# One core's decoder trunk: the compressed branch's pieces between the attention's groups, transposes at the changes of stage, and transfers in smaller pieces

## The chip, the cores and the metric

The kernel runs on one core of a Trainium2 chip. Its engines work side by side and wait for each other through semaphores: TensorE (PE; its weight loads are listed as PEld), VectorE (DVE), ScalarE (ACT), GpSimd (POOL) and SyncE (SP), which here only issues transfers. ACT issues transfers too. The metric is the device time of one execution in microseconds (us). TensorE's clock is granted by a throttle at one of two levels; the profile gives it as a share of full speed (PEclk).

## The reference

One layer on 512 prompt tokens and 8 sequences of 8 sample tokens, in float32: a half-step feed-forward layer (FFN), a mixer, a second half-step FFN, each between two RMS norms.

```
x = x + 1/2 * post1(SwiGLU_1(pre1(x)))
u = pre_m(x) @ w_in            # q, kv of three kinds, gates, z, xbc, dt
a = NSA(q, kv, gates)          # compressed + selected + window attention, gated
s = SSD(z, xbc, dt)            # causal convolution, chunked scan, grouped norm
x = x + post_m(concat(attn_norm(a), s) @ w_out)
x = x + 1/2 * post2(SwiGLU_2(pre2(x)))
```

The compressed branch (`compress_blocks` with the weights `w_cmp`) makes one key and one value of each block of 64 tokens; its softmax is added to the result of the two other branches. For the samples keys and values come from paged caches.

## The kernel before, in words

`x` is held transposed in `xT` (features on partitions, 8 chunks `k` of 576 tokens). Every float32 product of the large layers is made of three products of rounded parts: ACT writes the high part of an operand (rounded), VectorE subtracts it from the operand to get the low part, PE multiplies high by high, high by low and low by high (`product`, L490).

The stages follow each other, each a block of instruction streams, one per engine, in an order written by hand; a block begins when all engines have ended the one before. `setup` loads constants and pages of the sample's cache and compresses the pages (L399; a page is a transfer of 256 KB in rows of 2 KB, and the weights `w_cmp` come whole in two transfers of 2 MB in rows of 32 KB, L291 and L311). `ffn` is called twice; pieces of the weights are loaded to a ring, rounded by ACT (L750) and finished by VectorE (L811). `mixer_in` has two blocks: the first makes keys, values and gates (L984 to L1016), the second q, xbc and z. Then come `ssd`, `attend_prompt`, `attend_sample` and `mixer_out`.

Where a stage ends with a norm, the sum of squares is finished by the next stage: `tail.post.total` (L517) on PE, the root by ACT as Ln and Exp (L535 to L541), then for each chunk VectorE's `tail.scale` (L553) and `tail.add` (L558), ACT's rounding (L1034, L763) and VectorE's low part (L1057, L815), which PE waits for. VectorE's order there is scale 0, scale 1, add 0, scale 2, add 1, low part 0, and so on.

At the end of `mixer_in` VectorE copies the last rows of the convolution (L1279), which SP sends out. At the end of `ssd` SP sends the last state (L1376) and waits until it has landed.

`attend_prompt` has a prelude and a loop over 32 groups (kv head, branch, 128 queries). The prelude holds the lengths of the SSD rows, the compress of the prompt's keys and values, and the whole compressed branch: scores, a turn of them, softmax on VectorE and ACT, a turn of the shares, and products with the values (L1939), which are the first contents of the result `onat`. In the loop PE makes scores, turns them and multiplies by values; VectorE scales the result of a group to `tmp`, and POOL adds it to `onat`.

`mixer_out` begins with ACT's length of an attention row (L2737) and the rounding of the SSD rows and of the first weights (L2731, L2727; VectorE L2775, L2770).

## Time and profile before

| | |
|---|---|
| median of 3 runs | 1972.95 us (1970.59 to 1973.65) |
| profiled execution | 1965.59 us, span of its instructions 1963.7 |
| mean granted clock of TensorE | 0.947 |
| transfers | 189.15 MB, 96 GB/s in the mean |

The span is the time from the first to the last instruction of the profiled execution. Busy time counts an engine's arithmetic alone. A wait is put down to what ended it. "issue" and "PEq" as the releaser mean that no other engine's work or transfer was seen to end the wait, as with a barrier between blocks. A matmul's duration includes the way through the array, so that durations of neighbours overlap.

### The profile page before, as it was taken

The page shows a single profiled execution, that of the slowest core. Times are in us where ns is not written, and L with a number is a line of the kernel's source. Part 1 is how long each engine was busy: PE and PEld are TensorE (multiplying, and loading weights), DVE is VectorE, ACT ScalarE, POOL GpSimd, SP SyncE. Part 2 cuts the span into 40 slices and gives each one's busy share as a digit, 9 for nine tenths or more (in the row PEclk, how much of TensorE's full clock was granted, in tenths as well). Part 3 has the DMA queues.
Part 4 walks back from the last instruction along what each step waited for, and adds up shares of the span by engine and source line. Part 5 has one row for each costly group of instructions (what it writes and reads, how often), then busy time and mean ns, then how long its engine had stood idle before and what let it go on. Part 6 is the DMA issues. An engine that isn't in the chain of part 4 may idle for free. (4 is left out here: it accounts for less than half of the span.)

```text
span 1963.7 us, 36443 instructions
## 1 busy us (share of the span) xinstructions
PE 1772.0 (90%) x15067; PEld 1670.4 (85%) x15067; DVE 789.3 (40%) x1460; ACT 605.2 (31%) x967; POOL 111.9 (6%) x141
## 2 busy tenths in 40 slices
PE   3899999999978989997976999788897899999997
PEld 2789999999978989996755888666896899999996
DVE  3123443432242124744555555443525344443223
ACT  0122222222133212223434776243523322222222
POOL 0000000000000000101200111333000000000000
PEclk9899999999989989997977999899898999999998
DMA  9703444342311332321242002465320222223221
GB/s 252 272 26 116 145 150 152 112 121 76 88 48 44 92 92 75 86 54 40 83 124 71 23 23 65 145 200 151 102 86 22 65 85 85 85 85 95 78 84 48
DMA packets 256209, 189.15 MB, mean 96 GB/s; under 512 B 29604, under 2 KB 227744, under 8 KB 255299
## 3 DMA queue, kind: packets, MB, share of 16 engines
q1 hardware_dynamic: 248184, 173.43, 30.2%
q10 hardware_dynamic: 7916, 14.18, 2.5%
q8 instruction: 79, 1.29, 0.3%
q14 instruction: 30, 0.25, 0.0%
HBM read 176.14 MB, written 24.81 MB: 102 GB/s over the span
## 5 line engine op out<-in xcount | busy, mean ns | idle before, releaser
L490 PE MATMUL PS<-f_x_h,f_w_h 128*128 128x288 f32 x1408 | 303.6, 297 | 21.8 <-DVE f_w_l L811 12.1
L490 PE MATMUL PS<-f_x_h,f_w_l 128*128 128x288 f32 x1408 | 300.9, 295 | 0.0
L490 PE MATMUL PS<-f_x_l,f_w_h 128*128 128x288 f32 x1408 | 300.9, 295 | 0.0
L490 PEld LDWEIGHTS PS<-f_x_h,f_w_h 128*128 128x128 f32 x1408 | 227.9, 190 | 24.7 <-DVE f_w_l L811 13.3
L490 PEld LDWEIGHTS PS<-f_x_l,f_w_h 128*128 128x128 f32 x1408 | 227.4, 190 | 0.0
L490 PEld LDWEIGHTS PS<-f_x_h,f_w_l 128*128 128x128 f32 x1408 | 227.2, 189 | 0.0
L750 ACT CAST f_w_h<-f_raw 128x1024 fp32r<-128x1024 f32 x88 | 92.1, 1048 | 412.7 <-PE PS L490 334.1
L490 PE MATMUL PS<-f_h_h,f_out_w_h 128*128 128x288 f32 x704 | 150.9, 296 | 0.0
L490 PE MATMUL PS<-f_h_l,f_out_w_h 128*128 128x288 f32 x704 | 150.7, 295 | 0.0
L490 PE MATMUL PS<-f_h_h,f_out_w_l 128*128 128x288 f32 x704 | 150.7, 296 | 0.0
L811 DVE TENSOR_TENSOR f_w_l<-f_raw,f_w_h 128x1024 fp32r<-128x1024 f32 x88 | 107.7, 1225 | 50.0 <-ACT f_w_h L750 50.0
L807 DVE TENSOR_TENSOR f_out_w_l<-f_out_raw,f_out_w_h 128x1408 fp32r<-128x1408 f32 x32 | 52.0, 1625 | 188.3 <-ACT f_out_w_h L744 188.3
L490 PEld LDWEIGHTS PS<-f_h_h,f_out_w_h 128*128 128x128 f32 x704 | 113.4, 189 | 0.0
L490 PEld LDWEIGHTS PS<-f_h_l,f_out_w_h 128*128 128x128 f32 x704 | 113.2, 188 | 0.0
L490 PEld LDWEIGHTS PS<-f_h_h,f_out_w_l 128*128 128x128 f32 x704 | 112.8, 188 | 0.0
L490 PE MATMUL PS<-mk_x_h,mq_w_h 128*128 128x288 f32 x448 | 97.1, 299 | 8.7 <-DVE mq_w_l L1199 8.7
L744 ACT CAST f_out_w_h<-f_out_raw 128x1408 fp32r<-128x1408 f32 x32 | 43.9, 1371 | 179.1 <-PE PS L490 168.1
L490 PE MATMUL PS<-mk_x_l,mq_w_h 128*128 128x288 f32 x448 | 96.7, 298 | 0.0
L490 PE MATMUL PS<-mk_x_h,mq_w_l 128*128 128x288 f32 x448 | 96.5, 297 | 0.0
L399 PE MATMUL PS<-arena 64*64 64x64 f32 (+2 forms) x1536 | 75.7, 376 | 21.4 <-DMA arena<-in_cache_cmp_kv 13.0
L843 DVE TENSOR_TENSOR f_silu<-PS,norm_rows 128x576 f32<-128x576 f32 x44 | 33.3, 756 | 147.8 <-PE PS L490 139.6
L399 PEld LDWEIGHTS PS<-arena 64*64 64x64 f32 x1536 | 69.2, 167 | 27.6 <-issue 23.6
(405 smaller groups left out, 3107.0 us busy)
## 6 DMA issues: line engine op xcount, KB each, us to landing
f_raw<-in_ffn_w_in SPq DMA_DIRECT2D x88, 512.0 KB, 3.9
f_out_raw<-in_ffn_w_out SPq DMA_DIRECT2D x32, 704.0 KB, 4.6
arena<-in_cache_slc_kv SPq DMA_DIRECT2D x64, 256.0 KB, 3.1
mq_raw<-in_w_in SPq DMA_DIRECT2D x20, 512.0 KB, 3.8
arena<-in_cache_cmp_kv SPq DMA_DIRECT2D x32, 256.0 KB, 13.5
arena<-in_cache_cmp_kv ACTq DMA_DIRECT2D x32, 256.0 KB, 13.2
arena<-in_cache_win_kv SPq DMA_DIRECT2D x8, 1024.0 KB, 7.1
mo_raw<-in_w_out SPq DMA_DIRECT2D x16, 512.0 KB, 3.7
```

The source lines that it names most:

```text
L399: m = pe.matmul(PS[col:col + 64, 2 + 2 * c + half, c0:c0 + n], wd[r, c * HD + d + odd, :], rhs, start=(d == 0), stop=(d == HD - 2))
L490: m = pe.matmul(PS[:, bank + half, 0:HALF], a[:, wk, :], b[:, xk, half * HALF:(half + 1) * HALF], start=start and j == 0, stop=stop and j ...
L744: act.copy(ow[s].h, pieces.raw[s]).then_inc(o_h[s], 1)
L750: act.copy(ws[side].h, raw[side]).then_inc(s_h[side], 1)
L807: dve.tensor_tensor(ow[s].l, pieces.raw[s], ow[s].h_f32, ALU.subtract).then_inc(o_l[s], 1)
L811: dve.tensor_tensor(ws[side].l, raw[side], ws[side].h_f32, ALU.subtract).then_inc(s_l[side], 1)
L843: dve.tensor_tensor(cut(silu[j]), both(4 * j), cut(rstd[:, :]), ALU.mult).then_inc(s_gate, 1)
```

## The change

It has these parts. A helper `keep_turning` lets PE transpose the identity into a bank of the accumulator memory that nobody reads: 25 times at the start of each FFN, 30 before the final transposes, 40 at the start and 25 at the end of `mixer_in`, 20 at the end of `ssd`, 25 at the end of `attend_sample` and 25 at the start of `mixer_out`. In setup the two transfers of `w_cmp` become sixteen. The order on VectorE at the start of the second FFN and of `mixer_in` becomes scale 0, add 0, scale 1, low part 0, and so on. The two blocks of `mixer_in` become one (its ACT and VectorE streams are joined; the variables of the second are renamed to `q_ws`, `q_mm`, `q_ev`), and the convolution's rows are copied after the third z step. The waits for outgoing data at the end of `ssd` and `attend_sample` move into the next stage. In `attend_prompt` the weights come in quarters, only the compress itself stays ahead of the loop, and the compressed branch's pieces stand at the ends of groups 0 to 30, all through the one bank `BK`. VectorE then writes the first branch of a group straight to `onat` (`results`), the second goes by POOL as before, and the compressed values are added by VectorE. The sample's score matmuls for the new columns take both branches at once. In `mixer_out` ACT rounds before it takes row lengths.

```diff
-                    sp.dma_start(wd[0:64, :, :], kh).then_inc(s_w, 16)
+                    for j in range(8):
+                        sp.dma_start(wd[0:64, 16 * j:16 * j + 16, :], kh[:, 16 * j:16 * j + 16, :]).then_inc(s_w, 16)
...
-                        act.dma_start(wd[64:P, :, :], kh).then_inc(s_w, 16)
+                        for j in range(8):
+                            act.dma_start(wd[64:P, 16 * j:16 * j + 16, :], kh[:, 16 * j:16 * j + 16, :]).then_inc(s_w, 16)
...
+
+        def keep_turning(pe, bank, n):
+
+            for _ in range(n):
+                pe.transpose(PS[:, bank, 0:P], ident, ident)
...
                     if tail is not None:
                         tail.post.total(pe)
+                    keep_turning(pe, 5, 25)
...
                     if last:
                         post_norm.total(pe)
+                        keep_turning(pe, 5, 30)
...
                         rest_of_piece(1, 0)
                     for k in range(KD if rows is None else 0):
                         if tail is None and k == 1:
                             rest_of_piece(1, 0)
                         if tail is not None:
-                            tail.scale(dve, k)
-                            if k:
-                                tail.add(dve, k - 1)
-                            if k > 1:
-                                rest_of_x(k - 2)
-                        else:
-                            rest_of_x(k)
-                    if tail is not None:
-                        tail.add(dve, KD - 1)
-                        for k in range(KD - 2, KD):
+                            if k == 0:
+                                tail.scale(dve, 0)
+                            tail.add(dve, k)
+                            if k == 0:
+                                rest_of_piece(1, 0)
+                                rest_of_x(0)
+                            if k + 1 < KD:
+                                tail.scale(dve, k + 1)
+                        if tail is None or k:
                             rest_of_x(k)
                     if pages is not None:
...
+        def load_cmp(eng, half, q):
             w = io["w_cmp"].rearrange("a l c d e -> (a l) (c d) e")
-            for q in range(2):
-                eng.dma_start(wd[64 * half:64 * half + 64, :, :].rearrange("p (c d) e -> p c d e", c=2)[:, :, 32 * q:32 * q + 32, :],
-                              w.rearrange("l (c d) e -> l c d e", c=2)[:, :, 32 * q:32 * q + 32, :]).then_inc(s_cmp_w[q], 16)
+            eng.dma_start(wd[64 * half:64 * half + 64, :, :].rearrange("p (c d) e -> p c d e", c=2)[:, :, 16 * q:16 * q + 16, :],
+                          w.rearrange("l (c d) e -> l c d e", c=2)[:, :, 16 * q:16 * q + 16, :]).then_inc(s_cmp_w[q], 16)
...
                 @block.tensor
                 def _(pe):
                     tail.post.total(pe)
+                    keep_turning(pe, 5, 40)
...
+                    keep_turning(pe, 7, 25)
...
+                    act.wait_ge(s_sw, 32)
+                    act.copy(sw.h, smw).then_inc(s_swh, 1)
+                    nrm.take_root(act, 4, KD)
+                    round_piece(1)
...
+                        if p + 2 < NP:
+                            round_piece(p + 2)
+                        if p == NP - 2:
+                            act.wait_ge(s_wl, NP)
+                            for s in range(2):
+                                round_chunk(s, 0, land_q[s], 32)
+                    act.dma_start(stn, io["state_conv"].rearrange("a b w n -> (a b w) n")).then_inc(s_in, 16)
...
+                    tail.scale(dve, 0)
+                    for k in range(KD):
+                        tail.add(dve, k)
+                        if k + 1 < KD:
+                            tail.scale(dve, k + 1)
+                        rest_of_x(k)
...
-                    dve.wait_ge(s_lt, 1)
-                    for b in range(3):
-                        dve.tensor_copy(rows[:, 512 * b:512 * b + 512], PS[0:27, 4 + b, :]).then_inc(s_row, 1)
+                        if i == 2:
+                            dve.wait_ge(s_lt, 1)
+                            for b in range(3):
+                                dve.tensor_copy(rows[:, 512 * b:512 * b + 512], PS[0:27, 4 + b, :]).then_inc(s_row, 1)
 
...
                     sp.dma_start(out["p_ssm"][0, 0].rearrange("(k e) p n -> (e p) k n", e=2), h0[2]).then_inc(s_out, 16)
                     outs[0] += 1
-                    sp.wait_ge(s_out, 16 * outs[0])
...
                         m.then_inc(S["pst"], 1)
+                    keep_turning(pe, 0, 20)
...
+            ADDED = {13: (1, 0), 14: (1, 1), 15: (0, 0), 16: (0, 1), 21: (2, 0), 22: (2, 1), 29: (3, 0), 30: (3, 1)}
+            added = {u: n for n, u in enumerate(ADDED.values())}
...
                 def _(sp):
-                    load_cmp(sp, 0)
+                    for q in range(2):
+                        load_cmp(sp, 0, q)
...
+                        if kv == 0:
+                            for q in range(2, 4):
+                                load_cmp(sp, 0, q)
...
+                    def compressed_values(kv, two):
+                        n = added[kv, two]
+                        pe.wait_ge(S["kl"], 2 * {0: 3, 1: 3, 2: 4, 3: 4}[kv])
+                        if n:
+                            pe.wait_ge(C["oc"], n)
+                        r = slice(32 * kv, 32 * kv + 32)
+                        for i in range(2 * two, 2 * two + 2):
+                            m = pe.matmul(PS[:, BK, 256 * (i % 2):256 * (i % 2) + 256], pT[r, i, :],
+                                          vb[r, :, :].rearrange("p g d -> p (g d)"), start=True, stop=True)
+                        m.then_inc(C["o"], 1)
...
                     kt_transposes(pe, 6, nat[0:NS, 2, 4, :]).then_inc(S["kt0"], 1)
                     kt_transposes(pe, 1, nat[0:NS, 1, 4, :]).then_inc(C["kt"], 1)
                     keys(0, 0)
-                    state_lengths()
+                    state_lengths(0)
                     keys(0, 1)
                     pe.wait_ge(S["ktc"], 2)
                     pe.wait_ge(C["ktc"], 2)
-                    compress()
-                    pages_of_halves()
-                    compressed_scores()
-                    pe.wait_ge(C["vt"], 2)
-                    pe.matmul(PS[:, 6, 64:64 + HD], vc[:, :, :, :].rearrange("p h g n -> p (h g n)"), stack, start=True, stop=True).then_inc(C["vr"], 1)
-                    turned_scores()
-                    pe.wait_ge(C["x"], 1)
+                    state_lengths(1)
                     for g in range(3):
                         scores(0, g)
-                    pe.wait_ge(C["root"], 4)
-                    compressed_values()
+                    compress()
                     scores(0, 3)
-                    pe.wait_ge(C["oc_a"], 4)
-                    pe.wait_ge(C["oc_d"], 4)
+                    pages_of_halves()
...
+                        if G == 1:
+                            values_of_pages()
+                        if G in (2, 5):
+                            compressed_scores(G // 5)
+                        if G in (6, 7):
+                            turned_scores(G - 6)
+                        if G == 10:
+                            turned_shares()
+                        if G in ADDED:
+                            compressed_values(*ADDED[G])
...
                             act.wait_ge(S["s"], 4 * PER_KV * (kv - 1))
+                        elif kv:
+                            act.wait_ge(s_out, 16 * outs[0])
                         act.copy(q2[e][half(e), g, :], qT[half(e), 4 * (kv // 2) + g, 0:SEQ]).then_inc(S["qh"], 1)
...
+                        if G == 2:
+                            act.wait_ge(C["s"], 1)
+                            act.copy(sT[:, 0, :], PS[:, BK, :]).then_inc(C["sc"], 1)
+                        if G == 8:
+                            act.wait_ge(C["x"], 1)
+                            act.activation(sc[:, :, :], sc[:, :, :], ACT.Exp).then_inc(C["e"], 1)
+                        if G == 10:
+                            act.wait_ge(C["pt"], 1)
+                            act.copy(pT[:, :, :].rearrange("p i n -> p (i n)"), PS[:, BK, :]).then_inc(C["ptc"], 1)
...
-                        dst = onat[:, i, 4 * kv * HD:4 * (kv + 1) * HD].rearrange("p (g d) -> p g d", g=GQA)
-                        pool.wait_ge(S["m"], G + 1)
-                        if G:
-                            pool.wait_ge(S["ad"], G)
-                        pool.tensor_tensor(dst, dst, tmp[G % 2], ALU.add).then_inc(S["ad"], 1)
+                        if br:
+                            pool.wait_ge(S["m"], G + 1)
+                            if kv:
+                                pool.wait_ge(C["oc"], added[kv, i // 2] + 1)
+                            pool.tensor_tensor(results(kv, i), results(kv, i), tmp[i % 2], ALU.add).then_inc(S["ad"], 1)
...
+                    def add_compressed(kv, two):
+                        n = added[kv, two]
+                        dve.wait_ge(C["o"], n + 1)
+                        if kv:
+                            dve.wait_ge(S["m"], PER_KV * kv + 2 * two + 2)
+                        else:
+                            dve.wait_ge(S["ad"], 2 * two + 2)
+                        dst = onat[:, 2 * two:2 * two + 2, 256 * kv:256 * kv + 256]
+                        dve.tensor_tensor(dst, dst, PS[:, BK, :].rearrange("p (i n) -> p i n", i=2), ALU.add).then_inc(C["oc"], 1)
...
+                        if G == 0:
+                            pages_placed()
+                        if G == 1:
+                            values_by_head()
+                        if G == 5:
+                            dve.wait_ge(C["s"], 2)
+                            dve.tensor_copy(sT[:, 1, :], PS[:, BK, :]).then_inc(C["sc"], 1)
+                        if G in (6, 7):
+                            biased(G - 6)
+                        if G == 7:
+                            below_largest()
+                        if G == 9:
+                            shares()
+                        if G in ADDED:
+                            add_compressed(*ADDED[G])
+                        if 17 <= G < 25:
+                            state_norm(G - 17)
...
-                    for k in range(2):
-                        sp.wait_ge(s_og[k], 16 * DEC_BATCH // 2)
...
-                        for br in range(2):
-                            for p in range(2):
-                                m = pe.matmul(PS[:, 0, NS * br:NS * br + NS], qbd[:, b, p, :], ktn[:, br, p, :], start=(p == 0), stop=(p == 1))
+                        for p in range(2):
+                            m = pe.matmul(PS[:, 0, 0:2 * NS], qbd[:, b, p, :], ktn[:, :, p, :], start=(p == 0), stop=(p == 1))
                         m.then_inc(S["sw"], 1)
...
+                    keep_turning(pe, 5, 25)
...
+                    sp.dma_start(grow, bass.AP(io["att_out_norm"].tensor, 0, [[0, P], [1, ATT_WIDTH]])).then_inc(S["grow"], 16)
+                    for k in range(2):
+                        sp.wait_ge(s_og[k], 16 * DEC_BATCH // 2)
                     sp.dma_start(onat[0:NS, 4, :], scr_o.ap()[:, :]).then_inc(S["ld"], 16)
-                    sp.dma_start(grow, bass.AP(io["att_out_norm"].tensor, 0, [[0, P], [1, ATT_WIDTH]])).then_inc(S["grow"], 16)
...
+                    keep_turning(pe, 7, 25)
...
-                    length(0)
-                    state_rows(range(2))
+                    state_rows(range(1))
                     round_piece(0)
-                    state_rows(range(2, 8))
-                    length(1)
+                    state_rows(range(1, 8))
                     round_piece(1)
+                    for i in range(2):
+                        length(i)
+                    round_piece(2)
                     for i in range(2, 5):
                         length(i)
```

## Rows read from the trace of the kernel before

**Rows 1.** The page, part 1, busy time of each engine over the span
```profile
PE 1772.0 (90%) x15067; PEld 1670.4 (85%) x15067; DVE 789.3 (40%) x1460; ACT 605.2 (31%) x967; POOL 111.9 (6%) x141
```

**Rows 2.** Waits of PE: line, releaser: us in total, times, longest
```profile
PE PS L399 <- DMA arena<-in_cache_cmp_kv: 13.0, 1, 13.0
...
PE PS L490 <- DVE mo_w_l L2770: 10.6, 1, 10.6
PE PS L490 <- DVE f_x_l L815: 9.7, 1, 9.7
PE PS L490 <- DVE mq_w_l L1199: 8.7, 1, 8.7
...
PE PS L984 <- DVE mk_x_l L1057: 8.3, 1, 8.3
...
PE PS L1765 <- PEq L150: 7.8, 1, 7.8
...
PE PS L1421 <- PEq L150: 6.8, 1, 6.8
...
PE PS L993 <- DVE mk_sw_l L1073: 4.1, 1, 4.1
```

**Rows 3.** Six stretches at half clock: bounds, length, busy (instructions), PEclk
```profile
139.60:143.00 3.40, 2.89 (x12) 2.89 (x13) 2.51 (x6) 0.14 (x1) 0.00 (x0) 0.50 0.46 134
569.70:586.80 17.10, 8.49 (x28) 6.86 (x29) 12.29 (x15) 10.81 (x13) 0.00 (x0) 0.50 0.39 122
696.00:706.20 10.20, 4.19 (x17) 4.19 (x18) 2.40 (x3) 1.99 (x2) 0.00 (x0) 0.50 0.57 147
890.50:907.60 17.10, 13.05 (x94) 10.61 (x95) 6.40 (x13) 6.78 (x25) 3.70 (x5) 0.50 0.35 93
1375.20:1385.50 10.30, 2.87 (x12) 2.87 (x13) 5.58 (x8) 8.99 (x14) 0.00 (x0) 0.50 0.45 126
1494.70:1511.80 17.10, 7.38 (x23) 5.74 (x23) 12.35 (x16) 9.69 (x13) 0.00 (x0) 0.50 0.22 63
```

**Rows 4.** Timeline of PE, its transposes in setup and at the end
```profile
29.17 5.28 PE L377 MATMUL PS<-sq,arena 128*128 128x128 f32 x24 [10.82 <-issue]
...
1949.07 6.74 PE L732 MATMUL PS<-sq,xT 128*128 128x128 f32 x25 [5.08 <-DVE xT L558]
...
1957.46 1.43 PE L732 MATMUL PS<-sq,xT 128*128 128x128 f32 x10 [0.63 <-DVE xT L558]
```

**Rows 5.** Transfers issued between 0 and 100 us: size, us to landing
```profile
arena<-in_w_cmp SPq DMA_DIRECT2D x1, 2048.0 KB, 34.1
```

**Rows 6.** Two stretches of setup; the last column is GB/s
```profile
20.00:40.00 20.00, 7.57 (x42) 5.74 (x42) 6.95 (x15) 0.00 (x0) 0.00 (x0) 1.00 1.02 227
40.00:50.40 10.40, 0.04 (x4) 0.07 (x5) 0.00 (x0) 0.00 (x0) 0.00 (x0) 0.53 1.05 389
```

**Rows 7.** Timeline of VectorE, first FFN to mixer: start, us, line
```profile
578.21 0.81 DVE L553 SCALAR_TENSOR_TENSOR arena<-arena,gT,norm_rows 128x576 f32<-128x576 f32 x1
...
579.60 0.81 DVE L1057 SCALAR_TENSOR_TENSOR mk_x_l<-xT,gT,mk_x_h 128x576 fp32r<-128x576 f32 x1
```

**Rows 8.** Timeline of VectorE at the mixer's input's end
```profile
886.40 1.86 DVE L1279 COPY arena<-PS 27x512 f32<-27x512 f32 x3
```

**Rows 9.** Timeline of SP's queue at SSD's end
```profile
1013.00 0.38 SPq L1376 DMA_DIRECT2D out_p_ssm<-arena  x1
```

**Rows 10.** The prompt's attention: its prelude and its loop
```profile
1017.40:1068.20 50.80, 32.71 (x383) 22.13 (x383) 28.57 (x62) 22.51 (x37) 2.09 (x6) 0.67 0.50 125
1068.20:1237.40 169.20, 156.76 (x1232) 143.86 (x1232) 91.51 (x367) 115.99 (x223) 26.02 (x37) 0.99 0.10 32
```

**Rows 11.** Timeline of PE, values of the compressed branch
```profile
1064.65 2.09 PE L1939 MATMUL PS<-arena 32*128 32x256 f32 x16 [1.50 <-DVE arena L2252]
```

**Rows 12.** Groups of PE's instructions in the sample stage (mean ns)
```profile
L2433 PE MATMUL PS<-arena 128*128 128x64 f32 x64 | 8.0, 268 | 0.0
```

**Rows 13.** Timeline of ACT, start of the mixer's output
```profile
1376.48 1.06 ACT L2737 ACTIVATE arena<-arena 128x1024 f32<-128x1024 f32 x1 [6.40 <-PEq L150]
```

521 lines of the change are left out of this document (245 added, 276 removed).

## The prediction

> **What bounds the kernel now.** The page's busy shares first [rows 1]: TensorE (PE) works nine tenths of the span, the other engines under half, so the time is PE's own work plus the places where PE stands still plus the places where it runs at half clock. The view of PE's waits [rows 2] then gives the places: nearly all long waits are single ones, one at each change of stage, 7 to 13 us each, and the engine named is the one that prepares the next stage's first operand. Third, the granted clock of the stretches behind those waits [rows 3]: 0.50 of full speed, 1.2 in place of 2.4 GHz, from within the pause until some us into the new work. A matmul there costs double, so a pause is paid twice. The change goes at both, and its terms are taken seam by seam. No stage's steady part is touched, except the prompt's attention.
>
> **The price of a turn.** In setup 24 transposes of 128x128 back to back took 5.28 us, 0.22 each; near the end of the program 25 took 6.74 us at half clock (paced by VectorE), and the ten last 1.43, 0.14 each with the tail of the last [rows 4]. So I take 0.22 at half clock and half of it, 0.11, at full: 20, 25, 30 and 40 turns are 2.2, 2.7, 3.3 and 4.4 us at full clock, 4.4, 5.5, 6.6 and 8.8 at half. Between the 6.74 and the 1.43 PE did nothing but transposes, and the clock rose: turning can bring it up. A turn is free where PE waits longer than that, and holds the next stage (or a block's barrier) back where it doesn't.
>
> **Setup.** SP's half of the compress weights, one 2 MB transfer whose rows are 32 KB, landed 34.1 us after its issue [rows 5]. While it was under way the queues moved 227 GB/s; behind it, with 2 KB page rows alone, 389 [rows 6]. PE's first compress matmul waits 13.0 us for data [rows 2]. Cut in eight with rows of 4 KB, the 4.2 MB should go at a rate between these two. At 389 they and the pages behind them are through some 12 us sooner; at 227 nothing is gained, and seven more issues on each of the two queues cost up to 4 us of delay for the pages. The rate follows the rows' size in this trace, so I lean to the gain: -8.5 (-12 to +4). The Trainium skill, "DMA: Bandwidth & Descriptors", section Bandwidth, speaks against it: it advises batching to 1 MiB and more for three quarters of the peak, and these pieces are 256 KB. By it the term would be zero or a loss. The page loads behind them are 256 KB each as well and reach 389 GB/s [rows 6], so I let the row decide.
>
> **Start of the first FFN.** The 25 turns stand there too. PE's work in the 3.4 us at half clock is 2.89 [rows 3], of which half, 1.45, can be had; the turns end about 0.3 after the operand is ready: -1.2 (-1.5 to +2.5, if they run at half).
>
> **First FFN to the mixer.** PE waits 8.3 us for the first rounded x, and 4.1 more, a stage later, for the small weights' low part [rows 2]. VectorE's new order puts the first x two operations earlier: the scale at 578.21 and its add lead to the low part at 579.60 [rows 7], 1.4 us for the two. The small weights are rounded before the root instead of behind it, which takes the 4.1 off entirely, and the 3.4 us at half clock that follow that second pause (1.6 of gain, estimated like the one above). Of 8.49 us of PE work at half clock in the first stretch [rows 3], 2.2 are the old total that stays; half of the rest is 3.1. Sum -10.2. The 40 turns start when the total is out, 8.3 less 1.4 before x is ready in the new order, and take 4.4 to 8.8: a delay of up to 2 is possible (-6.5 to -11).
>
> **Inside the mixer's input.** Its two blocks become one. The wait of 8.7 us for the first q chunk [rows 2] was a barrier behind the outgoing transfers, then ACT's rounding and VectorE's subtraction; in the new order both run under the last two pieces of the kv product, and the transfers have nobody waiting. What's late next is nothing: PE goes straight on. A hand-off of 0.5 may stay: -8.2. Its 4.19 us at half clock [rows 3] give 2.1: -10.3 (-8 to -10.8).
>
> **Mixer's input to SSD.** Of the 6.8 us gap [rows 2], VectorE's 1.86 for the convolution's rows [rows 8] and SP's transfers behind them leave the end (they go three z steps earlier, where VectorE is half idle). The 25 turns, 2.7, then hold the barrier, and I take -2.5. The 13.05 us at half clock behind it [rows 3] would give 6.5 if the clock stayed up all through; it is a stage of short matmuls between waits, so I take 1.5: -4 (-1 to -7.5).
>
> **SSD to the prompt's attention.** SP sends the last state at 1013.00 [rows 9] and waits for it; PE waits 7.8 [rows 2]. The wait moves to a later copy of ACT's, long after the landing. The 20 turns, at half clock there, end about 1014; barrier and start follow: -2.3 (0 to -3).
>
> **The prompt's attention.** Its prelude is 50.8 us in which PE is busy 32.7 at a mean clock of 0.67; its loop is 169.2 with 156.8 busy [rows 10]. 32.7 at 0.67 is 21.9 at full clock. The compressed branch's scores, transposes and values, about 5 of these, leave for the loop; 17 stay, with about 9.5 of waits (first squares from ACT, weights of the compress). New prelude 26.5, so -24.3. The loop then gets: values, where 16 products of four row groups took 2.09 at half clock, twice, behind a wait of 1.50 for the bank [rows 11]. If the four ran beside each other, separate calls cost four times the 2.1 at full clock, 8.4; if not, 2.1. I take 6.8, near the upper end since a row group alone uses a quarter of the array. With 3 for scores and transposes that's 10, and 14 visits of a single bank, PE to VectorE or ACT and back: between nothing and that 1.50 each; groups of other work lie between, so some 0.2, 3 in all. Together -11.3 (-5 to -18).
>
> **Sample.** 64 matmuls of 64 columns, 8.0 us [rows 12], become half as many of 128; a column costs the same, the start of each is saved: -1 (0 to -2).
>
> **Sample to mixer's output.** PE waits 10.6 [rows 2]. In ACT's order the row length of 1.06 [rows 13] no longer stands ahead of the first operand, nor the table load behind it, by its place about as long; of the barrier, the wait for the samples' output goes, but the first 25 turns hold it to near its old end, and I take 1.4. Together -3.6; the 2.87 at half clock [rows 3] give 1.4: -5 (-2 to -6). The second 25, begun with the block, fit by 0.2 at full clock and overrun by 2.4 at half.
>
> **Second FFN.** PE waits 9.7 [rows 2] for x. Two scales and an add leave the path, 0.7 each by [rows 7], and the second piece's subtraction now fills VectorE's wait for ACT's rounding, 0.8: -3.0. Of 7.38 at half clock [rows 3], 2 is the total that stays; half of the rest 2.6: -5.6 (-2.5 to -7).
>
> **End.** 30 turns, 6.6 us, while PE waits for the residual; its transposes are paced by VectorE there [rows 4]: 0.
>
> **Sum:** -8.5 -1.2 -10.2 -10.3 -4 -2.3 -11.3 -1 -5 -5.6 = -59.4 against the profiled execution's 1965.59: 1906.2. That execution lies 7.4 under the median of the runs shown, which I add: 1913.6, forecast 1914.
>
> **The rivals.**
> *Turning doesn't raise or hold the clock.* Then the clock terms go (1.45, 4.7, 1.5, about 2 in the prelude, 1.4, 2.6), nearly 14, and the turns at half clock delay the mixer by up to 2 and the output by 2.4: about 17, 1931. Against it stand the transposes of [rows 4], after which the clock was up. The Trainium skill, "TensorE: Matmul & The Clock Gate", Part 4: PE-mode transpose, says that full clock does not engage for transposes, which don't count as busy in the same way; by that rule this rival is right. The setup and end rows disagree with it here, so 0.08.
> *The loop gives the prelude's gain back.* PE takes its work in order, so each visit of the bank may stall the scores behind it; with 11 us more of these, 0.8 a visit, the gain in the prompt is nil: 1925. For it: VectorE is busy over half of the loop and ACT two thirds [rows 10]. 0.17.
> *The weights in pieces gain nothing* (the queues' rate is then set by something other than the rows): 1922. 0.10.
> *Slower: each visit costs a whole group.* VectorE reaches its part of a visit only at the end of its group's work. The wait for the bank in the prelude was 1.50 [rows 11], and at that the change is still faster by 40; a group lasts 169.2/32 = 5.3 [rows 10]. At 14 visits the whole gain of 59 (and the 3 already counted) is gone from 4.4 each; at 5.3 it's 74 less 3, 1985. Against it: between a producer and its reader the order leaves one or more groups. 0.05.
> *Nothing comes of it,* since what ends each wait is another transfer that the profile doesn't name: 0.02 for within 0.2% (4 us, about what a measurement of this kernel can tell from none).
>
> **How the numbers follow.** The forecast has 0.55, the four rivals above 0.08, 0.17, 0.10 and 0.05, no change 0.02, and 0.03 is for turns that outlast several waits, 1930. Ends of the terms taken together would reach from 1894 to 1954; all late ends at once are unlikely, so the range is 1895 to 1941, which takes in the three rivals on the fast side. Faster 0.93, the same 0.02, slower 0.05.
>
> **What would show it.** Granted clock 1.00 behind each seam of [rows 3]; no wait at the q chunk; no wait for the small weights; first compress matmul before 44 us; a prelude under 30 us; a loop of 180 to 184, with waits in it under 1 us. Wrong, if the loop passes 190, if the low stretches stay, or if the new waits at the seams are the turns themselves.

## The result, and the profile after

The changed kernel takes 1925.68 us, median of four runs (1921.44 to 1929.51), beside 1972.28 for the kernel before in the same comparison (1970.59 to 1973.65, four runs): a ratio of 0.9764, 95% interval 0.9741 to 0.9786. It is 46.6 us faster by the medians. The profiled executions are 40.4 apart (1965.59 and 1925.17), because that of before lies some 7 under its median; the seams below add up to that 40.4.

First the page, busy shares and the clock by slices, to be set beside [rows 1].

```profile
span 1923.4 us, 36783 instructions
...
PE 1795.9 (93%) x15250; PEld 1697.0 (88%) x15250; DVE 792.3 (41%) x1464; ACT 603.6 (31%) x963; POOL 100.0 (5%) x125
...
PEclk8999999999999999998888999799999999999998
```

PE is still what fills the span, and the granted clock is 0.960 in the mean (0.947 before). Stretches at half clock, added up over the span, fell from 209.6 us to 152.4 (127.5 in a second profiled execution of the changed kernel).

PE's waits, which answer to [rows 2]: line waited at, releaser, and the sum, the count and the longest in us.

```profile
PE PS L401 <- DMA arena<-in_cache_cmp_kv: 15.4, 1, 15.4
...
PE PS L492 <- DVE f_w_l L820: 7.6, 2, 5.0
...
PE PS L1888 <- ACT arena L2056: 6.2, 1, 6.2
...
PE PS L492 <- DVE f_x_l L824: 3.8, 1, 3.8
PE PS L1980 <- DVE arena L2187: 3.2, 4, 1.7
...
PE PS L1901 <- DMA arena<-in_w_cmp: 2.9, 1, 2.9
...
PE PS L1029 <- DVE mk_x_l L1172: 2.2, 1, 2.2
PE PS L500 <- PEq L279: 2.2, 1, 2.2
...
PE PS L1764 <- PEq L150: 1.9, 1, 1.9
...
PE PS L1419 <- PEq L150: 1.5, 1, 1.5
```

The wait of 8.7 for the q chunk is gone, and so is that for the small weights' low part; the waits at the mixer, the SSD and the prompt's start are 1.5 to 2.2 where they were 7 to 8. Part of each is now turning, which the view counts as work. Two waits are new or stand out: 6.2 at L1888 in the prompt's prelude, and four at L1980 in its loop.

The clock behind three of the seams of [rows 3], in windows of about the same place and length (columns: window, its length, busy time and count of PE, weight loads, VectorE, ScalarE and GpSimd, granted clock, DMA share, GB/s).

```profile
563.60:577.30 13.70, 9.20 (x57) 8.33 (x58) 8.79 (x10) 9.36 (x11) 0.00 (x0) 0.84 0.62 173
1340.00:1350.30 10.30, 8.96 (x76) 8.52 (x74) 5.99 (x10) 6.03 (x10) 0.00 (x0) 1.00 0.44 130
1457.00:1470.70 13.70, 9.43 (x46) 8.13 (x46) 8.95 (x12) 9.12 (x12) 0.00 (x0) 0.75 0.27 78
```

These are the mixer's start, the output's and the second FFN's. The clock is up, but at two of the three not all through.

The seams one by one. Each number is the distance, on PE's timeline, between the end of a stage's last product and the start of the next one's first, or within a stage from its first to its last, in us. The second FFN's start is counted from the first product of the sum of squares ahead of it; setup from the start of the span; the prompt's loop begins at the same scores in both.

| Step of the prediction | Before | After | Change | Forecast |
|---|---|---|---|---|
| setup, to the last compress product | 135.60 | 129.19 | -6.4 | -8.5 |
| start of the first FFN, with its body | 4.51 + 426.9 | 6.28 + 427.3 | +2.2 | -1.2 |
| first FFN to mixer, with the kv part | 13.59 + 112.70 | 12.58 + 104.04 | -9.7 | -10.2 |
| inside the mixer's input: q chunk, then q to z | 8.74 + 183.68 | 0.65 + 182.02 | -9.7 | -10.3 |
| to the SSD, with the SSD | 6.75 + 117.22 | 4.18 + 115.84 | -4.0 | -4 |
| SSD to the prompt | 7.79 | 6.03 | -1.8 | -2.3 |
| prompt: prelude and loop | 50.8 + 169.2 | 30.7 + 183.7 | -5.6 | -11.3 |
| sample | 131.93 | 134.98 | +3.1 | -1 |
| sample to output, with the output | 10.60 + 109.2 | 7.13 + 107.7 | -5.0 | -5 |
| second FFN, start and body | 11.75 + 433.17 | 9.09 + 431.90 | -3.9 | -5.6 |
| end | 19.50 | 19.95 | +0.5 | 0 |

They sum to -40.3 against the -59.4 of the prediction. Four steps hold 15 of the 19 that are missing: the prompt 5.7, the sample 4.1, the first FFN's start 3.4, setup 2.1.

This is one execution on each side, and stages repeat less well than seams. In the executions kept here (the experiments' too), stages whose code an experiment left as changed took: the prompt 209.3 to 221.5 us, the sample 128.8 to 141.0, the SSD 112.0 to 116.6, the second FFN's body 431.9 to 440.1. A row of a few us in these is not yet an effect. The waits at the seams repeat within 1 to 2 us.

### The profile page after: what moved, and what is told of

It reads as the page before. It is cut to its first block and busy times, and to the rows that moved or that the text cites. A ratio compares the mean times of both kernels' runs of the same rounds, so it can differ in the third digit from the quotient of the medians.

```text
span 1923.4 us, 36783 instructions
## 1 busy us (share of the span) xinstructions
PE 1795.9 (93%) x15250; PEld 1697.0 (88%) x15250; DVE 792.3 (41%) x1464; ACT 603.6 (31%) x963; POOL 100.0 (5%) x125
## 5 line engine op out<-in xcount | busy, mean ns | idle before, releaser
L820 DVE TENSOR_TENSOR f_w_l<-f_raw,f_w_h 128x1024 fp32r<-128x1024 f32 x88 | 107.7, 1225 | 44.6 <-ACT f_w_h L759 44.6
L401 PE MATMUL PS<-arena 64*64 64x64 f32 (+2 forms) x1536 | 75.8, 376 | 22.7 <-DMA arena<-in_cache_cmp_kv 15.4
```

What stands on the lines that cost most here:

```text
L401: m = pe.matmul(PS[col:col + 64, 2 + 2 * c + half, c0:c0 + n], wd[r, c * HD + d + odd, :], rhs, start=(d == 0), stop=(d == HD - 2))
L820: dve.tensor_tensor(ws[side].l, raw[side], ws[side].h_f32, ALU.subtract).then_inc(s_l[side], 1)
```

## The experiments

Three questions: what the turning does to the clock and what it costs; where setup's gain comes from; and why the prompt's attention gave half of what was expected. The runs of the kernel before were taken anew with each group of experiments, with a median of 1967.08, 1970.99 and 1969.88 us. Ratios are to these.

### The changed kernel again, and without its turns

> The changed kernel itself, as the measure for the three others on the same chip: 1921 to 1930 us, 0.976 of the kernel before.

Measured: 1925.97 us (1915.76 to 1930.26, six runs), 0.9783 (0.9753 to 0.9813). This is the mark for the three that follow.

```diff
-            for _ in range(n):
+            for _ in range(0):
                 pe.transpose(PS[:, bank, 0:P], ident, ident)
```

> All turns of the identity are left out, the rest is as changed. If turning raises or holds the clock: long half-clock stretches come back at the first FFN's end, the second FFN's start and the mixer's output (some 17 us each where the changed kernel has two of 3.4), while the barriers at the first FFN's start and SSD's end come some 2 us sooner each; net 5 to 12 us slower than the changed kernel, about 1934. If transposes don't count for the clock: the half-clock stretches stay as they are with the turns, and the kernel is 4 to 6 us faster than the changed one, about 1920.

Measured: 1928.18 us (1921.26 to 1940.84), 0.9806 (0.9772 to 0.984): not told apart from the kernel with its turns. The windows at the same three seams, without turns:

```profile
563.60:577.30 13.70, 5.37 (x18) 4.25 (x19) 8.93 (x11) 8.91 (x11) 0.00 (x0) 0.50 0.57 162
1335.00:1345.20 10.20, 5.16 (x21) 5.17 (x22) 7.20 (x10) 8.08 (x13) 0.00 (x0) 0.50 0.45 133
1454.50:1464.70 10.20, 3.00 (x13) 3.03 (x14) 7.09 (x10) 7.14 (x10) 0.00 (x0) 0.50 0.36 103
```

All three are at half clock, 0.50 where the changed kernel had 0.84, 1.00 and 0.75 (its second execution has 0.79 at the second FFN): transposes of the identity do raise the clock here. That goes against the rule weighed in the prediction (the Trainium skill, "TensorE: Matmul & The Clock Gate", Part 4: PE-mode transpose), and the measurement decides.

The gain in time is small, and paid for elsewhere. The kv part took 105.31 without turns (104.04 with them), the output with its seam 116.17 (114.79): 2.7 us for the turns, in this pair of executions. With the same turns at these two places other executions took 102.4 to 105.3 and 114.8 to 116.5, so the gain lies between nothing and 4.3 and isn't shown to be more than scatter. Against it stand the seams that the turns lengthen: the first FFN's start 4.51 without (6.28, and 4.87 in the second execution), the SSD's 2.96 (4.18), the prompt's 4.86 (6.03 and 5.50), 2.2 to 4.2 together. The second FFN's start is 9.09 in both. No run puts the old orders back while it keeps the turns; that the orders brought the rest is read from the waits that are gone.

### Turns left out where they hold the next stage back

```diff
                         tail.post.total(pe)
-                    keep_turning(pe, 5, 25)
+                        keep_turning(pe, 5, 25)
...
                         m.then_inc(S["pst"], 1)
-                    keep_turning(pe, 0, 20)
```

The first line's new indent drops the turns at the first FFN, which has no total ahead of it, and keeps those at the second; the last drops those behind the SSD.

> The 25 turns at the first FFN's start and the 20 at SSD's end are left out. If these two hold a stage back (theory): the first FFN's first product comes 2.2 us sooner after the last compress product, the prompt's first transpose 1.5 to 2 us sooner after SSD's last, 3 to 4 us in all, 1922. If they are free or pay by the clock: no change or up to 3 us slower.

Measured: 1922.14 us (1909.44 to 1927.41), 0.9759 (0.9727 to 0.9791); the two seams are 4.50 and 4.87, as without any turns. The changed kernel's timeline shows why (start, duration, line, tile and shape, idle time ahead of it).

```profile
131.37 4.45 PE L500 MATMUL PS<-sq 128*128 128x128 f32 x25 [2.17 <-PEq L279]
135.47 0.74 PE L492 MATMUL PS<-f_x_h,f_w_h 128*128 128x288 f32 x2
...
567.78 5.36 PE L500 MATMUL PS<-sq 128*128 128x128 f32 x40
575.35 0.36 PE L1029 MATMUL PS<-mk_w_h,mk_x_h 128*128 128x256 f32 x1 [2.22 <-DVE mk_x_l L1172]
...
981.88 4.31 PE L500 MATMUL PS<-sq 128*128 128x128 f32 x20
988.12 0.68 PE L1764 MATMUL PS<-sq,arena 64*128 64x64 f32 x8 [1.93 <-PEq L150]
```

At 131.37 PE waits 2.17 for its own queue, turns for 4.45 us, and the FFN's first product follows with no wait: its operand was there before the turns ended. At 981.88 the 20 turns last 4.31, 0.22 each, so at half clock, ahead of a barrier. At 567.78 they end 2.22 us before the operand and cost nothing. The first FFN's body is 429.4 without its turns (427.3 with them), with half clock from 130.4 to 137.3, so what the seam saves (1.78) is given back (2.13). The medians of the two kernels differ by 4, inside their intervals.

### Turns long enough to reach the operand

```diff
-                        keep_turning(pe, 5, 25)
+                        keep_turning(pe, 5, 58)
...
-                    keep_turning(pe, 5, 40)
+                    keep_turning(pe, 5, 58)
...
                     keys(0, 0)
+                    keep_turning(pe, 0, 40)
                     state_lengths(0)
```

These three stand on top of the last experiment: at the second FFN, at the mixer and in the prompt's prelude. The theory was that the gap left between the last turn and the operand is what lets the clock fall again.

> As e3, and the turns at the mixer's start (58 in place of 40) and the second FFN's start (58 for 25) last until the first operand is there; 40 more stand in the prompt's prelude behind the first keys, where PE waited 6.2 us. If PE's being busy right up to the work is what holds the clock: the half-clock stretches of 3.4 us behind both starts go (1.7 us each) and most of the 10 us one in the prelude (2 us), 5 us less than e3, about 1917. If the fall of the clock does not depend on these pauses of 2 to 6 us: as e3, or slower by the turns that overrun.

Measured: 1926.46 us (1921.4 to 1930.13), 0.9787 (0.9761 to 0.9813): no gain. The mixer's seam is 12.48 (12.58 with 40 turns) and its kv part 104.04, as with 40 turns; the way to the loop's first values is 36.38 (36.42). At the second FFN, and then the stretch from the first product on, here and in the changed kernel:

```profile
1454.38 8.52 PE L500 MATMUL PS<-sq 128*128 128x128 f32 x58
1462.66 0.51 PE L492 MATMUL PS<-f_x_h,f_w_h 128*128 128x288 f32 x2
```
```profile
1462.70:1468.00 5.30, 5.30 (x36) 4.88 (x35) 5.07 (x8) 3.21 (x5) 0.00 (x0) 1.00 0.22 65
```
```profile
1466.60:1472.00 5.40, 5.40 (x25) 4.91 (x26) 5.13 (x8) 2.72 (x4) 0.00 (x0) 0.68 0.34 97
```

The clock does here what the theory said: it rises at 1458.5, in the midst of the transposes, and stays at 1.00 behind the first product, where eight of the nine executions with 25 turns have a stretch at half clock. But 58 turns outlast the wait, and the FFN starts 1.2 later (10.33 behind the start of the sum of squares, not 9.09), which takes back what the clock gives. In the prelude 13.7 us at half clock follow from 1004.6 all the same. So it is the worth of closing the gap that fell, not the theory for the clock, for which this is one execution.

### Products in place of transposes

```diff
-                pe.transpose(PS[:, bank, 0:P], ident, ident)
+                pe.matmul(PS[:, bank, 0:P], ident, ident, start=True, stop=True)
```

> As changed, with a plain float32 product of the identity by itself in place of each turn. If transposes count less than products for the clock, as the Trainium skill has it: the half-clock stretches of 3.4 us at both FFNs' starts, at the first FFN's end and at the mixer's start go, and none comes in the turns. If what lets the clock fall are the pauses before and behind the turns (theory): the same stretches as with transposes, and the barriers later where a product takes longer than a turn.

Measured: 1936.17 us (1933.92 to 1938.42, two runs), 0.983 (0.9776 to 0.9883). The clock at the mixer's start and at the second FFN's, and the 40 products at the mixer:

```profile
566.20:580.00 13.80, 13.12 (x86) 12.58 (x87) 9.02 (x10) 9.44 (x11) 0.00 (x0) 0.76 0.52 156
1464.00:1478.00 14.00, 9.91 (x72) 9.01 (x73) 9.14 (x12) 9.11 (x12) 0.00 (x0) 1.00 0.26 75
```
```profile
568.93 10.99 PE L500 MATMUL PS<-sq 128*128 128x128 f32 x80
```

A product of this type shows as two records, 80 for 40, and takes twice the time, so this is more turning as well as another kind. It outlasts the waits: the first FFN's start is 9.11, the mixer's seam 15.93, the SSD's 7.03. At the second FFN the clock is 1.00 where 25 transposes gave 0.75, which is what that rule of the Trainium skill would lead one to expect; but behind the first product 58 transposes gave 1.00 too (above), and at the mixer it is no higher than with transposes. Whether kind or length made the difference at the one seam stays open.

### Setup: whole weights, shorter rows, all partitions

The compress weights whole, as before:

```diff
-                    for j in range(8):
-                        sp.dma_start(wd[0:64, 16 * j:16 * j + 16, :], kh[:, 16 * j:16 * j + 16, :]).then_inc(s_w, 16)
+                    sp.dma_start(wd[0:64, :, :], kh).then_inc(s_w, 16)
...
-                    pe.wait_ge(s_w, 256)
+                    pe.wait_ge(s_w, 32)
```

> As changed, but setup's compress weights come whole again, in two transfers of 2 MB with rows of 32 KB. If the pieces brought the 6 us in setup (theory): the first compress product at 50 us in place of 45, the queues at 150 to 230 GB/s while the weights are under way, the first FFN's first product 5 to 6 us later, 1931. If they gained nothing and something else in setup moved: 45 us and the same time.

Each queue's half in 16 pieces with rows of 2 KB:

```diff
-                    for j in range(8):
-                        sp.dma_start(wd[0:64, 16 * j:16 * j + 16, :], kh[:, 16 * j:16 * j + 16, :]).then_inc(s_w, 16)
+                    for j in range(16):
+                        sp.dma_start(wd[0:64, 8 * j:8 * j + 8, :], kh[:, 8 * j:8 * j + 8, :]).then_inc(s_w, 16)
...
-                    pe.wait_ge(s_w, 256)
+                    pe.wait_ge(s_w, 512)
```

> As changed, with the weights in 16 pieces a queue, rows of 2 KB as the pages have. If the length of a row sets the rate (theory): 380 to 390 GB/s already while the weights are under way, where the changed kernel shows 225 to 300, and the first compress product at about 40 to 42 us, in spite of 8 more issues of 0.6 us on each queue. If it is that a weight transfer reaches half of the partitions only: the rate stays at 225 to 300, the first product at 45 to 47.

Pieces that go to all 128 partitions, four to a queue:

```diff
-                    for j in range(8):
-                        sp.dma_start(wd[0:64, 16 * j:16 * j + 16, :], kh[:, 16 * j:16 * j + 16, :]).then_inc(s_w, 16)
+                    for j in range(0, 4):
+                        sp.dma_start(wd[:, 16 * j:16 * j + 16, :], bass.AP(kh.tensor, kh.offset + 16 * j * HD, [[0, 2], [2 * HD * HD, 64], [1, 16 * HD]])).then_inc(s_w, 16)
...
-                    pe.wait_ge(s_w, 256)
+                    pe.wait_ge(s_w, 128)
```

> As changed, with rows of 4 KB, but each piece fills all 128 partitions (both halves from the same rows of memory), four pieces a queue in place of eight. If the partitions of a transfer set its rate: 380 to 390 GB/s and the first compress product at 40 to 42 us. If the length of a row does (theory): as changed, 45 us, less some 0.5 for the four issues saved.

Measured, in this order: 1930.03 us (1921.44 to 1935.48), 0.9779 (0.974 to 0.9819); 1921.72 (1914.4 to 1923.54), 0.9739 (0.9708 to 0.9769); 1987.59 (1984.37 to 1990.69), 1.0079 (1.0055 to 1.0103). PE's first compress product starts at 50.13, 42.94 and 111.74, beside 45.03 in the changed kernel and 50.36 before.

The queues while the weights are under way: in the changed kernel,

```profile
14.00:34.00 20.00, 12.74 (x65) 10.71 (x64) 12.07 (x26) 0.00 (x0) 0.00 (x0) 0.90 1.04 257
```

with whole weights,

```profile
14.00:34.00 20.00, 9.70 (x45) 8.69 (x46) 8.28 (x16) 0.00 (x0) 0.00 (x0) 1.00 1.05 221
```

with rows of 2 KB,

```profile
14.00:34.00 20.00, 12.13 (x63) 10.30 (x63) 11.51 (x25) 0.00 (x0) 0.00 (x0) 0.93 1.06 299
```

and, later, with the pieces to all partitions.

```profile
30.00:60.00 30.00, 0.00 (x0) 0.00 (x0) 0.00 (x0) 0.00 (x0) 0.00 (x0) 0.50 0.13 51
```

The last two columns are to be read: the engines are equally full in the first three, and 221, 257 and 299 GB/s go through them with rows of 32, 4 and 2 KB. Cutting is worth 5.1 us at the first product, and 4.8 at the last compress product (134.00 with whole weights, 129.19). Rows of 2 KB bring another 2.1 at the first product. Other executions with rows of 4 KB have it at 43.7 to 45.6, so 0.8 to 2.7; the last product comes at 127.6, and at 125.6 in the last experiment below, against 127.3 to 130.5. The medians alone don't tell 5 us from none. In these runs the rows and the pieces became smaller together, so which of the two sets the rate is not separated. The rule of the Trainium skill, "DMA: Bandwidth & Descriptors", section Bandwidth, that speaks for transfers of 1 MiB and more didn't hold at this place: pieces of an eighth and a sixteenth of the 2 MB were faster. The pages alone had 389 [rows 6], with rows of 2 KB too, so row length is only a part. Whether the other part is the 64 partitions that each half goes to was the third experiment's question, and it gave no answer: its transfers kept 0.13 of the engines busy, as much as two of sixteen, and starved PE.

### The prompt: the branch back in the prelude

The whole function of before (with POOL's additions too), with the changed kernel's loads in quarters:

```diff
-                    load_cmp(sp, 0)
+                    for q in range(4):
+                        load_cmp(sp, 0, q)
...
-                            if d % 32 == 0:
-                                pe.wait_ge(s_cmp_w[d // 32], 32)
+                            if d % 16 == 0:
+                                pe.wait_ge(s_cmp_w[d // 16], 32)
```

> As changed, but the prompt's attention is that of the kernel before: the whole compressed branch ahead of the loop, with the weights in quarters. If the spreading is worth what the traces show (prelude 20 us shorter, loop 14 longer): the stage is 5 to 8 us longer, 1932, with PE idle about 12 us in its loop. If the loop's pieces cost what the prelude gains and the quarters alone shorten the prelude: no difference. If the spreading is worth the forecast 11 us: 1937.

Measured: 1935.07 us (1930.81 to 1935.66), 0.9812 (0.9787 to 0.9837). Up to the loop's first products with the values, and from there to the loop's end, here and in the kernel before:

```profile
986.90:1045.40 58.50, 36.65 (x408) 25.90 (x409) 31.79 (x76) 25.55 (x45) 2.62 (x7) 0.68 0.40 113
1045.40:1209.00 163.60, 151.67 (x1208) 139.10 (x1206) 88.53 (x353) 112.82 (x217) 25.40 (x36) 1.00 0.11 33
```
```profile
1017.40:1073.80 56.40, 37.81 (x408) 26.87 (x409) 31.53 (x76) 25.69 (x45) 2.70 (x7) 0.67 0.45 113
1073.80:1237.40 163.60, 151.66 (x1208) 139.12 (x1206) 88.55 (x353) 112.81 (x217) 25.40 (x36) 1.00 0.11 33
```

The quarters alone gain nothing, and the loop is as before. The two parts make 222.1 us, where the changed kernel has 36.4 + 177.9 = 214.3 (213.0 in its second execution). Spreading the branch is worth 8 to 9 beside these two; beside all eight executions with the changed function and its whole loads (209.3 to 221.5) it is 1 to 13. By the ratios it is 6 beside the repeated run, 9 beside the first result. The size is uncertain, but the loop does not give all of it back.

### Less to transfer in the prelude

```diff
-            eng.dma_start(wd[64 * half:64 * half + 64, :, :].rearrange("p (c d) e -> p c d e", c=2)[:, :, 16 * q:16 * q + 16, :],
-                          w.rearrange("l (c d) e -> l c d e", c=2)[:, :, 16 * q:16 * q + 16, :]).then_inc(s_cmp_w[q], 16)
+            eng.dma_start(wd[64 * half:64 * half + 64, :, :].rearrange("p (c d) e -> p c d e", c=2)[:, :, 16 * q:16 * q + 8, :],
+                          w.rearrange("l (c d) e -> l c d e", c=2)[:, :, 16 * q:16 * q + 8, :]).then_inc(s_cmp_w[q], 16)
```

Half of the prompt's compress weights isn't loaded.

> As changed, but each quarter of the prompt's compress weights brings only the first half of its columns (rows of 2 KB in place of 4), so half of the compress works with old contents; no instruction is left out. If the transfers set the prelude's end (theory; 221 GB/s with the queues full from its start to the last weights): the compress no longer waits (2.9 and 1.5 us), and the first products with the loop's values come 4 to 6 us sooner after the stage's start than the 36.4 of the changed kernel. If ACT's late first squares set it (PE waits 6.2 us for them): under 1 us.

Measured: 1926.69 us (1923.24 to 1930.14, two runs), 0.9782 (0.9728 to 0.9836). From the prompt's first product to the loop's first values it takes 29.78 where the changed kernel takes 36.42. PE's waits there:

```profile
PE PS L1888 <- ACT arena L2056: 5.7, 1, 5.7
...
PE PS L1901 <- issue: 1.0, 1, 1.0
```

The wait of 2.9 for the weights is gone, that for the first squares from ACT stays. In the changed kernel the stretch from the prompt's first product to the end of the transfers, and the one behind it, are

```profile
988.10:1013.00 24.90, 15.54 (x215) 11.92 (x216) 12.65 (x26) 17.84 (x29) 1.96 (x5) 0.79 0.96 221
1013.00:1024.50 11.50, 9.87 (x144) 8.55 (x132) 4.34 (x22) 3.40 (x9) 1.20 (x3) 0.55 0.30 94
```

with DMA engines 0.96 busy in the first, and PE near half clock in the second. The other executions of this prelude with whole loads take 32.9 to 36.7, so 3 to 7 us go with half of the transfer (6.6 beside the one shown): it has a part in setting the prelude's end, through PE's wait and through the half clock behind it. By the median nothing shows; in the profiled execution the sample took 141.0 (135.0) and the second FFN 438.9 (431.9), in code that the edit doesn't touch.

### The softmax's steps one at a time

In the loop, VectorE ran the whole maximum (`below_largest`) at the end of group 7 and the whole sum and gating (`shares`) at the end of group 9. Here each step stands by itself behind a minimum of groups 8 to 10.

```diff
...
+                            if (G, g) in softmax:
+                                softmax[G, g]()
...
-                        if G == 7:
-                            below_largest()
-                        if G == 9:
-                            shares()
```

> As changed, but VectorE's softmax of the compressed branch is no longer done in two runs of 1.6 and 2.4 us at the ends of groups 7 and 9: its steps stand singly between the minima of the scores of groups 8 to 10. If VectorE's runs make PE wait there (1.7, 0.6 and 0.5 us at the scores) and the clock falls in that pause (theory): these waits go below 1 us in all, the half-clock stretches 80 and 94 us after the stage's start go, and the loop is 172 to 175 us long in place of 178. If the clock falls there for another reason, or the steps only move the wait: the stretches stay and the loop is 176 to 179.

Measured: 1917.37 us (1912.21 to 1930.1), 0.9756 (0.9708 to 0.9804). What it was to remove, in the changed kernel: the whole loop from its first values, the stretch of `shares`, and the one behind it,

```profile
1024.50:1202.40 177.90, 168.11 (x1270) 150.18 (x1268) 105.58 (x385) 114.45 (x220) 13.12 (x19) 0.98 0.11 31
...
1075.00:1081.60 6.60, 4.62 (x35) 4.00 (x35) 6.36 (x17) 3.09 (x7) 0.00 (x0) 0.99 0.01 4
1081.60:1085.00 3.40, 3.40 (x19) 3.40 (x19) 1.85 (x9) 3.22 (x7) 0.00 (x0) 0.52 0.00 0
```

and on PE's timeline the wait at its end.

```profile
1079.21 0.50 PE L1980 MATMUL PS<-pa_kh,pa_q 128*128 128x512 f32 x1 [1.69 <-DVE arena L2187]
```

In this stretch VectorE is busy 6.36 of 6.60 us (2.4 of them the block itself), PE waits 1.69 for a minimum that stands behind the block, and then works 3.4 us at half clock without any further pause. The same happens at group 7 (half clock from 1067.9 to 1071.3). With the steps apart, the loop and its waits at that line are

```profile
1016.10:1188.70 172.60, 164.48 (x1270) 146.85 (x1268) 104.87 (x385) 114.60 (x220) 13.15 (x19) 1.00 0.11 32
```
```profile
PE PS L1980 <- DVE arena L2187: 0.9, 2, 0.5
```

The count of instructions is the same, the clock 1.00 in place of 0.98, the time 172.60 in place of 177.90: 5.3 us, 3.6 of them PE's busy time and the rest waits. But the clock doesn't always fall behind the blocks. The kernel with rows of 2 KB in setup has the same blocks, and its loop and its waits at that line are

```profile
1019.30:1194.20 174.90, 164.89 (x1269) 146.91 (x1268) 105.13 (x385) 114.22 (x219) 13.13 (x19) 1.00 0.11 31
```
```profile
PE PS L1980 <- DVE arena L2187: 3.1, 4, 1.7
```

The same pause of 1.69 us stands in it, and the clock is 1.00 throughout. Of ten profiled executions with the blocks two have no half clock in the loop (175.0 us from the first values), the others 3.4 to 23.9 us of it behind a block (176.3 to 184.9); the two with the steps apart have none (172.6 both). So some 2.4 us are gained without the clock, and the rest only where the clock would have fallen. The medians of the two kernels overlap.

### The better parts together

Rows of 2 KB in setup, the softmax's steps apart, and turns only at the start of `mixer_in` (40) and of `mixer_out` (25); no other edit.

> As changed, with three edits: setup's weights in rows of 2 KB, VectorE's softmax spread as in e9, and turns only at the mixer's start and the output's. Setup gains 1 to 2 us, the loop 3 to 5, the barriers at the mixer's end and SSD's 2 and the sample's 1, so 7 to 10 us less than the changed kernel, 1916 to 1919, if the single gains add up; 1922 to 1926 if the clock takes them back elsewhere.

Measured: 1917.2 us (1902.63 to 1920.98, six runs), 0.9721 (0.9681 to 0.9761), the lowest ratio of all, though its interval overlaps that of the changed kernel. The first compress product starts at 42.06, the first FFN's seam is 4.52, the SSD's 2.96, the prompt's 4.88, the loop 172.60. It is no faster by its median than the spread softmax alone: its profiled execution has half clock for 13.7 us in the SSD, 20.5 in the sample and 17.1 at the end.

## Why the prediction came out as it did

The direction and the range were right (1895 to 1941), the forecast of 1914 was 12 too low. In the profiled executions, from which its terms come, the miss is 19: 1906.2 forecast, 1925.17 measured. The prediction added 7.4 because the execution of before lay that far under its median; the changed kernel's lies 0.5 under its own. So 7 of the 19 were made up by luck.

1925.68 is the very time that the rival "the loop gives the prelude's gain back" named, but that mechanism did not occur. The prelude and the loop in the changed kernel, with the boundary of [rows 10]:

```profile
988.10:1018.70 30.60, 19.75 (x320) 15.38 (x320) 13.21 (x29) 18.11 (x30) 2.90 (x8) 0.74 0.78 181
1018.70:1202.40 183.70, 173.76 (x1298) 155.26 (x1296) 109.37 (x405) 117.59 (x226) 13.38 (x20) 0.97 0.12 36
```

PE's idle time in the loop fell, from 169.2 - 156.8 = 12.4 to 183.7 - 173.8 = 9.9, so the visits of the single bank cannot have stalled it by 11. The agreement is an accident of several smaller misses.

Of the signs that the prediction named, three came (at the q chunk only a hand-off of 0.7, no wait for the small weights, a loop of 180 to 184). Four did not: the clock behind the seams is 0.84, 1.00 and 0.75, the first compress product comes at 45.03 and not before 44, the prelude is 30.7 and not under 30, and one wait in the loop is 1.7. And of its signs of being wrong one came at one place: at the first FFN the turns are themselves the wait.

**Right in place and size.** First FFN to mixer (9.7 of 10.2), the q chunk (8.1 of 8.2 for the hand-off), mixer's input to SSD (4.0 of 4), SSD to prompt (1.8 of 2.3), sample to output (5.0 of 5). What they have in common is that the wait's last releaser was moved in the order of an engine that had time, and its old cover was read off the trace. The sizes at the mixer are luck in part: 3.1 of the 10.2 were put to the turns, but without any turns 8.4 of the 9.7 stay. At the output 3.6 stay, which is what the step had without the clock.

**The prompt's prelude, mis-sized: 26.5 forecast, 30.7 measured.** The step counted 17 us of work at full clock and 9.5 of waits. PE was busy for 19.75, of which 8.0 at half clock, and idle for 10.85. The work was not more than counted (15.7 at full clock); the 2.7 of busy time beyond the 17 are the clock, which the step took as full and which is 0.74, and 1.4 of the miss are waits (6.2 for the first squares, 2.9 and 1.5 at the weights). The queues are full for 25 of the 31 us: the branch no longer stood in the way, and the transfer of the weights did in part; halving it took off 3 to 7.

**The loop: its length nearly right, its terms not.** Ten of work and 3 of hand-offs were forecast, 14.5 came: busy time rose by 17, idle time fell by 2.5. In the execution without half clock in the loop (rows of 2 KB) busy time from the first values on is 164.9 where it was 151.7 before: 13.2 of added work at full clock, 3 more than forecast (the values alone show 9.0 in place of 6.8). Some 3 more are half clock behind the two softmax blocks, which was not foreseen. The 3 for hand-offs were wrong in kind: what cost was not the bank, but VectorE's block of several steps at one place.

**Start of the first FFN, failed.** The step let the turns end 0.3 behind the operand, as 25 at full clock from the place where the compress ends. They begin after 2.17 us of PE's own queue and take 4.45, so they set the start: +1.8 in one execution, +0.4 in the other. The clock term of 1.45 is not seen against the kernel before (the body took 426.9, and 427.3 after); against the kernel without turns, whose body is 428.8, it is 1.5.

**Setup, mis-sized: 6.4 of 8.5.** The rate came out between the two rows, 257 GB/s, nearer to the low one. The cause is as forecast for 4.8 of the 6.4, as the whole weights show; the rest is within what the same setup differs by. The wait of 15.4 for a page is longer than the 13.0 of before though it ends 5.3 sooner, since PE's work ahead of it ended 7.8 sooner.

**Second FFN, mis-sized: 3.9 of 5.6.** The start gained 2.65 of 3.0; of the 2.6 for the clock at most 1.3 is in the body, which is less than that body differs between executions of one kernel (431.9 and 439.0). Here both sides have the shorter kind of body.

**Sample, failed: +3.1 in place of -1.** The fewer, wider matmuls did save their time: the 64 of [rows 12] at 8.0 us became 32 at 4.9. But the stage's clock was 0.90 (0.93 before): the work that follows the pause at its start ran at half clock for 20.5 us, for 10.2 before, on the same instructions. The second execution has half clock for 10.2 us at that place and still takes 134.2, and other executions, with edits far from the stage, give 128.8 to 141.0. So which part of the step failed stays open, and that it is an effect of the change is not settled.

**The turns.** That they raise the clock was right; that this is worth some 14 us was not. The clock terms were read as half of the work at half clock; what the turns add over the new order is 2.7 in the pair of executions compared and between nothing and 4.3 in others, less what they hold back. The medians with and without them are 2.2 apart, inside their scatter.

## What to carry to other kernels

Move the last releaser of a seam's wait into the work that precedes it; at the q chunk that took off 8.1 of 8.7 us, while work invented to keep the clock up raised the clock and gained nothing here that the medians can tell, and held the next stage back where it outlasted the wait. When a branch is spread over a busy loop, break its steps on the slower engine up too: two blocks of 1.6 and 2.4 us there stopped PE for up to 1.7, and in eight of ten executions the clock fell behind one of them. Read rates of loads by their rows and pieces: cutting one 2 MB transfer with 32 KB rows moved the same bytes faster, in pieces so small that one would have expected the opposite. And before a difference of a few us in one stage is called an effect, look at that stage in other executions with the same code: here the prompt and the sample differed by 12.

## What was not expected of the hardware

A pause as short as 1.69 us, in a loop in which PE is 95% busy, was followed by 3.4 us at half clock (the window from 1081.6 above), and with the whole weights, behind the same two blocks, by 6.8 from 1068.3 and 17.1 from 1081.9. With rows of 2 KB in setup the same pause at the same place was followed by none. Which pauses do this and which don't is open.

Transfers whose source has a first dimension of 2 kept 0.13 of the DMA engines busy, as much as two of sixteen, and moved 51 GB/s.

The FFNs run at two speeds with PE 100% busy and the clock at 1.00 in both. The first FFN and the second, 200 us each, in the changed kernel,

```profile
200.00:400.00 200.00, 200.00 (x1502) 200.00 (x1501) 84.08 (x95) 52.38 (x64) 0.00 (x0) 1.00 0.42 133
1600.00:1800.00 200.00, 200.00 (x1533) 200.00 (x1532) 77.66 (x84) 50.02 (x58) 0.00 (x0) 1.00 0.31 89
```

and in its second profiled execution:

```profile
200.00:400.00 200.00, 200.00 (x1540) 200.00 (x1540) 85.81 (x98) 52.37 (x64) 0.00 (x0) 1.00 0.43 135
1600.00:1800.00 200.00, 200.00 (x1503) 200.00 (x1503) 75.82 (x81) 48.61 (x56) 0.00 (x0) 1.00 0.29 84
```

1502 matmuls in one, 1540 in the other, of the same instructions, and the first FFN's body takes 427.3 and 420.5 us. That is a swing of 7 us per FFN, as large as most edits here. The faster speed stands in three of the 28 FFN stages kept (the second of the kernel before, and these two), so it can be a part only of the 10 to 20 us by which a kernel's runs scatter; nothing here shows its cause.
